# Decoder layer on one core: projections as single float32 products, expert slots filled from phase one on, cache values loaded 128 partitions wide

## The reference, cut to what matters

```python
u = x @ w_in + b_in                    # columns: lru_x 1024 | lru_y 1024 | q 1024 | k 256 | v 256 | gates 2 x 1024
rec = recurrent_branch(lru_x, lru_y)   # conv width 4, two block gates, scan over time, * gelu(lru_y)
att = window_attention(q, k, v)        # 16 heads, 4 kv heads, window 128; the samples read cache_k and cache_v
merged = sigmoid(g_l) * (rec @ w_lru_out) + sigmoid(g_a) * (att @ w_attn_out)
x1 = layer_norm(ALPHA * x + merged @ w_o)
# hierarchical MoE: best of 4 groups, two best of its 8 experts
y = layer_norm(ALPHA * x1 + sum_over_2_experts(w * (silu(x1 @ w_gate[e]) * (x1 @ w_up[e])) @ w_down[e]))
```

## Time and profile before

| | us |
|---|---|
| median of 3 runs (1116.97 to 1119.11) | 1118.64 |
| profiled execution, first to last instruction (span) | 1115.6 |
| PE busy | 936.1 |
| DVE busy | 403.5 |
| ACT busy | 267.6 |
| start of the first expert's first transpose | 593.65 |

### The profile page before, as it was taken

How to read it: one execution, slowest core, us unless ns; L and a number is a source line. 1 busy time by engine, 2 the same in 40 slices (tenths; PEclk the granted TensorE clock), 3 DMA queues, 4 the chain that set the end, 5 groups by cost and what they waited for, 6 DMA issues and landing times.

```text
span 1115.6 us, 14382 instructions
## 1 busy us (share of the span) xinstructions
PE 936.1 (84%) x5619; PEld 631.1 (57%) x5619; DVE 403.5 (36%) x874; ACT 267.6 (24%) x508; POOL 120.9 (11%) x195
## 2 busy tenths in 40 slices
PE   7999952999999999999927998888887887887844
PEld 6999952888999998978823333322222222222311
DVE  4765831776564545265561111010110011001126
ACT  3556430444344342311110111100110011011111
POOL 3000401000000000000012122011111111110003
PEclk8999985999999999999957999999999999989986
DMA  9233440211122142723494899999999999999962
GB/s 290 76 77 76 127 96 21 75 42 52 62 77 76 55 135 77 195 100 137 176 416 179 336 422 420 422 421 424 422 422 421 423 424 423 420 422 423 422 243 112
DMA packets 87896, 268.84 MB, mean 241 GB/s; under 512 B 32657, under 2 KB 59405, under 8 KB 67330
## 3 DMA queue, kind: packets, MB, share of 16 engines
q1 hardware_dynamic: 77602, 254.89, 58.8%
q0 software_dynamic: 10240, 13.21, 3.6%
HBM read 263.17 MB, written 15.16 MB: 249 GB/s over the span
## 4 chain that ended last, share of the span: by engine, by line
PE 50%; DMA 27%; DVE 10%; SPq 4%; another core or an unknown queue 3%; ACT 3%; issue 2%; POOLq 0%; POOL 0%; DVEq 0%; ACTq 0%
DMA slot<-in_w_up 26%; PE ps L764 25%; PE ps L1066 7%; PE ps L1093 5%; PE ps L981 5%; SPq L459 4%; PE ps L851 2%; PE ps L805 1%; PE ps L885 1%; DVE rawL L1450 1%; PE ps L875 1%; DVE hL L1536 1%; PE ps L1049 1%; PE ps L1001 1%
## 5 line engine op out<-in xcount | busy, mean ns | idle before, releaser
L1066 PE MATMUL ps<-slot,xt 128*64 128x512 f32 x512 | 248.3, 634 | 71.5 <-DMA slot<-in_w_up 70.5
L1067 PE MATMUL ps<-slot,xt 128*64 128x512 f32 x512 | 248.6, 635 | 0.0
L1066 PEld LDWEIGHTS ps<-slot,xt 128*64 128x64 f32 x512 | 69.3, 144 | 222.1 <-issue 152.8
L764 PE MATMUL ps<-xTh,wh 128*128 128x260 f32 x704 | 149.4, 294 | 1.5 <-DVE rawL L1450 1.5
L764 PE MATMUL ps<-xTl,wh 128*128 128x260 f32 x704 | 144.0, 287 | 0.0
L764 PE MATMUL ps<-xTh,rawL 128*128 128x260 f32 x704 | 144.0, 286 | 0.0
L1928 DVE COPY xt<-ps 128x512 f32<-128x512 f32 x32 | 22.1, 692 | 295.8 <-PE ps L1049 295.8
L1093 PE MATMUL ps<-slot,hT 128*64 128x512 f32 x512 | 116.9, 598 | 1.4 <-DVE hT L1938 1.4
L764 PEld LDWEIGHTS ps<-xTh,wh 128*128 128x128 f32 x704 | 112.4, 194 | 2.8 <-issue 1.8
L764 PEld LDWEIGHTS ps<-xTl,wh 128*128 128x128 f32 x704 | 111.5, 194 | 0.0
L764 PEld LDWEIGHTS ps<-xTh,rawL 128*128 128x128 f32 x704 | 110.9, 193 | 0.0
(11 more groups left out here) (314 smaller groups left out, 1210.2 us busy)
## 6 DMA issues: line engine op xcount, KB each, us to landing
slot<-in_w_down SPq DMA_DIRECT2D x32, 2048.0 KB, 28.7
slot<-in_w_gate SPq DMA_DIRECT2D x64, 1024.0 KB, 27.8
slot<-in_w_up SPq DMA_DIRECT2D x64, 1024.0 KB, 32.4
raw<-in_w_in SPq DMA_DIRECT2D x18, 1024.0 KB, 5.1
raw<-in_w_in SPq DMA_DIRECT2D x16, 256.0 KB, 4.5
raw<-in_w_lru_out SPq DMA_DIRECT2D x4, 1024.0 KB, 5.1
raw<-in_w_attn_out SPq DMA_DIRECT2D x16, 256.0 KB, 4.6
wo_raw<-in_w_o SPq DMA_DIRECT2D x4, 1024.0 KB, 8.6
```

What stands on the lines that cost most here:

```text
L764: last = mm(out_of[:, a, 0:HT], w[:, k, :], x[:, k, a * HT:(a + 1) * HT], start=(k == 0 and n == 0), stop=(k == KT - 1 and n == 2))
L1066: mm(out[0:CAP, :], tokens, w[:, q, :], start=start, stop=stop)
L1067: last = mm(out[CAP:P, :], tokens, w[:, 4 + q, :], start=start, stop=stop)
```

## The change

- **Products.** `passes` becomes `product`: one float32 product per block and half, 16 matmuls to a tile, straight from `raw`. `w_hi`, `w_lo`, `wo_hi`, `wo_lo` and the splits of the activations are gone, with their semaphores; ACT and DVE copy the transposed x in turns. `mix` has 16 matmuls to a token tile. The factor 0.5 that was folded into `w_o` moves into the layer norm (`2.0 * ALPHA` and a second epsilon).
- **Buffers.** `raw` has four buffers instead of three. `m1`/`mg`, `sg`, `wo`, `kwin`, `snew`, `lnG`, `lnB`, `xre` and `x1T` lie elsewhere, which leaves some expert slots free from the start or from tile 44 on.
- **Expert slots.** `chunk(0, 0, 0)` is issued behind half-chunk 8, `chunk(1, 1, 1)` and `chunk(2, 1, 1)` behind half-chunks 25 and 26, three chunks at the last merge, and expert 2's three chunks when the last token tile's sum is ready. All of `w_o` is loaded behind the last half-chunk.
- **Cache values.** `cV` is loaded 128 partitions wide; its row 0 is written afterwards, behind the conv state stores and a wait of POOL for the load. DVE's wait in `probs_t` for the stores and the loads is gone, and so is ACT's wait for the h store before the first gate tile.

```diff
-AHEAD = 3
+RAWS = 4
-for _k in range(KT):
-    _place(FIRST["ga"] + 11 + _k // 2, ("wo", _k))
...
             for hc in range(2, NT // 2):
                 half_chunk(hc)
-                if hc == 24:
-                    sp.wait_ge(s_proj, FIRST["lo"] + 12)
-                    for n in range(2):
-                        sp.dma_start(wo_raw[0][:, 2 * n:2 * n + 2, :], w_o[:, 2 * n:2 * n + 2, :]).then_inc(s_wo, 16)
+                if hc == 8:
+                    chunk(0, 0, 0)
+                if hc == FIRST["ga"] // 2 + RAWS - 1:
+                    chunk(1, 1, 1)
+                if hc == FIRST["ga"] // 2 + RAWS:
+                    chunk(2, 1, 1)
             sp.wait_ge(s_pv, NUNIT)
             sp.wait_ge(s_pa, 2 * NUNIT)
+            sp.wait_ge(s_oc_out, 16 * 9)
+            sp.wait_ge(s_oh_out, 32)
...
             x_again(1)
+            chunk(1, 0, 0)
             chunk(2, 0, 0)
             chunk(0, 1, 1)
...
                 if m == TT - 1:
-                    sp.wait_ge(s_lg, 3)
-                    chunk(0, 0, 0)
-                    chunk(1, 1, 1)
                     sp.wait_ge(s_mix, TT)
-                    chunk(1, 0, 0)
+                    chunk(0, 2, 2)
+                    chunk(1, 2, 2)
+                    chunk(2, 2, 2)
...
-            def passes(out_of, hi, lo, rhs_h, rhs_l):
+            def product(out_of, w, x):
                 last = None
                 for k in range(KT):
-                    for n, (w, x) in enumerate(((hi, rhs_h), (hi, rhs_l), (lo, rhs_h))):
-                        for a in range(2):
-                            last = mm(out_of[:, a, 0:HT], w[:, k, :], x[:, k, a * HT:(a + 1) * HT],
-                                      start=(k == 0 and n == 0), stop=(k == KT - 1 and n == 2))
+                    for a in range(2):
+                        last = mm(out_of[:, a, 0:HT], w[:, k, :], x[:, k, a * HT:(a + 1) * HT],
+                                  start=(k == 0), stop=(k == KT - 1))
...
-                pe.wait_ge(s_hi, t + 1)
-                pe.wait_ge(s_lo, t + 1)
+                if t % 2 == 0:
+                    pe.wait_ge(*raw_full(t))
...
-                    lo = woL[k // 4][:, k % 4, :]
-                    for p, (x, w) in enumerate(((mgH, woH[:, k, :]), (mgH, lo), (mgL, woH[:, k, :]))):
-                        for h in range(2):
-                            last = mm(out[0:ROWS[n], h, :], x[:, k, cols], w[:, h * 512:(h + 1) * 512],
-                                      start=(k == 0 and p == 0), stop=(k == KT - 1 and p == 2))
+                    for h in range(2):
+                        last = mm(out[0:ROWS[n], h, :], mg[:, k, cols], wo[k // 4][:, k % 4, h * 512:(h + 1) * 512],
+                                  start=(k == 0), stop=(k == KT - 1))
```

More of the change, by code:

```diff
@@ L172, in build @@
         oh = at("oh", [NS + 1, D], F32, oF + 4096)
[L173 to L176, removed]
+        raw = [at(f"raw{n}", [P, KT, 256], F32, oG + 8192 * n) for n in range(RAWS)]
         xc = [at(f"xc{n}", [P, XCW], F32, oI + 2176 * n) for n in range(2)]
@@ L292, in build @@
         s_x = [sem(f"token_tile_loaded{n}") for n in range(TT)]
-        s_raw = [sem(f"raw_loaded{n}") for n in range(3)]
+        s_raw = [sem(f"raw_loaded{n}") for n in range(RAWS)]
         s_cst = sem("constants_built")
         s_xT = sem("x_transposed")
-        s_xh, s_xl = sem("x_hi"), sem("x_lo")
+        s_xa, s_xd = sem("x_T_by_act"), sem("x_T_by_dve")
         s_vT, s_col = sem("vectors_transposed"), sem("vectors_in_columns")
@@ L328, in build @@
         s_ln = sem("ln1_loaded")
-        s_wo = sem("w_o_loaded")
+        s_wo = [sem(f"w_o_loaded{n}") for n in range(2)]
         s_mix, s_z, s_sd = sem("sum_ready"), sem("ln_stats"), sem("ln_root")
@@ L360, in raw_full @@
             hc = t // 2
-            return s_raw[hc % 3], 16 * sum(dmas(n) for n in range(hc % 3, hc + 1, 3))
+            return s_raw[hc % RAWS], 16 * sum(dmas(n) for n in range(hc % RAWS, hc + 1, RAWS))
         def emptied(t):
@@ L367, in emptied, with wcol @@
             return (s_eva if who == "act" else s_evd), n
[L369 to L374, removed]
+        def wcol(t):
+            return raw[(t // 2) % RAWS][:, :, (t % 2) * P:(t % 2 + 1) * P]
         def halves(ap):
@@ L779, in tile @@
                 kind, i = TILES[t]
-                rhs_h, rhs_l = {"lo": (recH, recL), "ao": (attH, attL)}.get(kind, (xTh, xTl))
+                rhs = {"lo": rec, "ao": att}.get(kind, xT)
                 if t == 0:
-                    pe.wait_ge(s_xl, TT)
+                    pe.wait_ge(s_xa, 3)
+                    pe.wait_ge(s_xd, 2)
                 if kind == "lo" and i == 0:
@@ L892, in cache_t @@
                     pe.wait_ge(s_ck, 16)
-                    pe.wait_ge(s_attl, 1)
+                    pe.wait_ge(s_att, 1)
                     pe.wait_ge(s_pd, 2)
@@ L1150, in _ @@
             sc = nc.scalar
-            for n in range(TT):
+            for n in range(0, TT, 2):
                 r = ROWS[n]
                 act.wait_ge(s_xT, n + 1)
[L1154 to L1162, removed]
+                sc.activation(xT[:, :, n * P:n * P + r], flat[n % 2].rearrange("p (k c) -> p k c", k=KT)[:, :, 0:r],
+                              ACT.Copy).then_inc(s_xa, 1)
             def read_tile(t):
@@ L1292, in sample_att @@
                     for p2 in range(2):
[L1293 to L1297, removed]
+                        ins = sc.activation(att[half, 4 * p2:4 * p2 + 4, SEQ:T], o[half, p2, a, :, :], ACT.Copy)
+                    ins.then_inc(s_sat, 1)
             act.wait_ge(s_lam, 1)
@@ L1327, in _ @@
                     sample_att()
-                elif what == "wo":
-                    wo_hi(*args)
             def root_of(m, before):
@@ L1334, in root_of @@
                 act.wait_ge(s_z, before + m + 1)
-                sc.activation(mv[0:r, m % 3, 2:3], mv[0:r, m % 3, 1:2], ACT.Sqrt, bias=epsT[0:r, :]).then_inc(s_sd, 1)
+                eps = epsT[0:r, 0:1] if before else epsT[0:r, 1:2]
+                sc.activation(mv[0:r, m % 3, 2:3], mv[0:r, m % 3, 1:2], ACT.Sqrt, bias=eps).then_inc(s_sd, 1)
             def x1_t(m):
@@ L1674, in read_tile @@
                     link(v.scalar_tensor_tensor(out=yb[:, :], in0=y2[:, :], scalar=1.0, in1=yb[:, :], op0=ALU.add, op1=ALU.mult))
-                    link(v.scalar_tensor_tensor(out=yb[:, :], in0=yb[:, :], scalar=0.5, in1=hL[:, i, 0:T], op0=ALU.mult, op1=ALU.mult))
-                    link(v.tensor_copy(recH[:, i, 0:T], yb[:, :]))
-                    v.tensor_tensor(recL[:, i, 0:T], yb[:, :], recH[:, i, 0:T].bitcast(F32), ALU.subtract).then_inc(s_rec, 1)
+                    v.scalar_tensor_tensor(out=rec[:, i, 0:T], in0=yb[:, :], scalar=0.5, in1=hL[:, i, 0:T],
+                                           op0=ALU.mult, op1=ALU.mult).then_inc(s_rec, 1)
                 elif kind == "lo":
@@ L1727, in _ @@
                     probs_t(*args)
-                elif what == "pv":
-                    attend(*args)
                 elif what == "sk":
```

151 lines of the change are left out of this document (48 added, 103 removed).

## The result

The changed kernel takes 1157.65 us (median of 4 runs, 1156.97 to 1161.84) against 1118.23 of the kernel before (4 runs): ratio 1.037, 95% interval 1.034 to 1.039. The prediction was 941 us, between 924 and 970. It has the wrong sign.

A forecast was written before the change was run, and what follows sets the result against it. PE was taken to bound the path up to the experts, apart from the hole, and expert weight transfer the rest. Gains 36.2 + 36 + 17 + 42.8 + 27 + 19 = 178 off 1118.64 gave 941 us, range 924 to 970.

The forecast's parts named there:

- A tile becomes 16 x 0.219 = 3.50 us: Projections on PE: 16 float32 products at 0.219 us replace 48 float32r ones, gaining 2.25 us a tile.
- a float32 product costs four float32r ones: Rival for projections and sum with w_o: 0.482 us a product, so slower, 1215 us; chance 0.03.
- The hole: PE idle from 152.74 us, before tile 20, through DVE's wait for row 0 of cV; its removal gains 36.2 us.
- The price of a load that stays slow: Cache values: a 53 us cV load would hold POOL until 157 and DVE 20 us at tile 22: 961 us.
- Phase one's walk: Stretch-by-stretch estimate of gains from start to tile 59, with the limits set by DVE and ACT taken off.
- start and tiles 0 to 19: First projections, recurrence and unit 0's scores: gain 36 us, with 10 of 46 lost to DVE; tile 20 starts near 118.5.
- tiles 20 to 28: Tiles that are round trips of ACT and DVE: nine gain 2.2 each, less 3 for the clock; gain 17 us.
- tiles 29 to 47: Projections among attention matmuls: 19 tiles gain 2.25 us each, 42.8 us, up to 6 less if units slip.
- tiles 48 to 59: Last unbroken projections of phase one: 69.47 us becomes 42, gain 27 us.
- sum, norm and routing, up to the first transpose: Sum with w_o: 4.5 token tiles on the path gain 4.2 us each, 19 us; the way after the logits stays.
- DVE and ACT keep the pace of tiles 13 to 28: Rival in phase one: only the hole is gained in those tiles, 26 us lost, 967 us; chance 0.14.
- PE sets the pace everywhere: Rival in phase one: DVE's 17 us of scans hide behind four tiles, so 927 us; chance 0.12.

## Why the prediction was wrong, point by point

**The step that failed** is "A tile becomes 16 x 0.219 = 3.50 us". The price 0.219 was right for one instruction: 7.01/32. The count was not. I took the instructions in the trace for the products in the code. The rows of before could have told: the gate step writes four products (two weight matrices, two halves), and I read "8 in 1.83" as eight of them without counting the loop. The groups of the kernel before, by form, against what the code issues (44 tiles read x, so 44 x 16 = 704 float32r products of low x by high weights; 48 scores of 256 columns; 8 gates x 2 halves = 16 products with each gate matrix):

```profile
L764 PE MATMUL ps<-xTl,wh 128*128 128x260 f32 x704 | 144.0, 287 | 0.0
...
L851 PE MATMUL ps<-kz,qT 128*128 128x256 f32 x96 | 23.2, 385 | 0.0
...
L805 PE MATMUL ps<-xc,wrg 128*128 128x272 f32 x32 | 8.7, 393 | 0.0
```

A float32r product has one row (704 for 704); a float32 one has two (96 for 48, 32 for 16). A price per instruction was multiplied with a number of products. The right working from the same rows was 4 products in 1.83 us, 0.458 for 272 columns, 0.437 for 260; a tile 16 x 0.437 = 7.0.

**The break-even was named and crossed.** The text said that the change turns slower from about 0.39 us a product on; the product costs 0.438. The rival "a float32 product costs four float32r ones", chance 0.03, is the one that came, with its price a little high: 0.438 is 3.63 times 0.1206. At the granted clock of 1.00 (2.4 GHz) 0.438 us are 4.04 clocks a column, and a float32r product takes 1.11. The Trainium skill, FP8 and Floating Point Precision, section TensorE Precision Notes, says that true FP32 makes four passes. These rows agree with it, and my sentence that the rows did not show it was wrong, since I had read half a product. The rival's 1215 us was too slow as it kept 0.482 a product and gave nothing back for stalls.

**The sum over PE.** Tiles: 60 x 1.25 = 75 us more instead of 135 less. Sum with `w_o`: 12 more (4.5 token tiles) instead of 19 less. The hole gives 36 back. 75 + 12 - 36 = 51, and the first transpose moved by 38.3: the remaining 13 or so are what PE no longer loses to others. Its idle time before the experts fell from 77.6 to 34.7 us, 42.9, of which 34.4 are the wait of the hole, so 8.5 are other stalls. The rest, some 4 us, I did not separate; the granted clock is a candidate (0.98 from 190 to 420 us in the kernel before, 1.00 in the changed one).

**The hole** (36.2): right in size (35.8 measured with the load alone). The price of a load that stays slow, 20 us, was right in its way, POOL's queue and `qz`, and no run tests its size. The 20 and the 157 belong to tiles of 3.5 us. The run with the narrow load has tiles of 7.01; POOL stood there for 55 us, until 208, and it cost 10. Nor did POOL stand at the wait that the text had in mind: that run has none.

**Phase one's walk**, tested with half the products:

| part | gain predicted | gain with half the products |
|---|---|---|
| start and tiles 0 to 19 | 36 | 31.6 (154.5 to 122.97) |
| tiles 20 to 28 | 17 | 18.4 (80.0 to 61.6) |
| tiles 29 to 47 | 42.8 | 42.0 (150.9 to 108.9) |
| tiles 48 to 59 | 27 | 27.1 (69.47 to 42.35) |
| sum, norm and routing, up to the first transpose | 19 | 19.6 (102.6 to 82.9) |
| experts | 0 | -2.4 (522.0 to 524.3) |
| whole, with 36.2 for the hole | 178 | 172.5 (spans, 1115.6 to 943.1) |

The total fits within 6 us, and so does each part within 5. What is missing lies mostly in the first part: tile 20 starts at 122.97 for a forecast of 118.5. DVE's scans ended at 110.3 for 109, and behind the gap of 4.92 us the granted clock was 0.69 (111.8 to 119.0): unit 0's scores took 2.07 us there, and the tile behind them 4.72 for 3.5. "DVE and ACT keep the pace of tiles 13 to 28" (967) and "PE sets the pace everywhere" (927) would have been wrong with these tiles.

**The early chunks and the experts**: worth 0 and 522 us; right (1157.04 for 1157.65 without the early chunks, 523.3 us for the experts).

## What to carry to other kernels

When a price per instruction is read from a trace and multiplied with a count from the code, count one known loop on both sides first: here 16 products written stood against 32 rows, and that factor of two was nearly the whole error: with half the products the kernel takes 944 us, for a forecast of 941. On these rows three float32r products (0.36 us for 260 columns) are cheaper on PE than one float32 product (0.44), so the split pays here, where PE is the bound in phase one and the other engines have room for it. The gain from a removed wait could be had alone: the wide load without the rest gives 36 us and beats both kernels.

## What the runs showed of the hardware that I had not expected

- A float32 product is two matmuls with two weight loads in the trace, each some 2 clocks a column: 0.219 us for 260 columns and 0.434 for 512, so 0.438 and 0.868 for the product; a float32r one took 0.1206 and 0.232.
- The 127-partition load of 1 MB not only landed late (53.5 to 57.1 us for the row behind it, against 8.6 to 11.8 for the load and 1.7 to 4.0 for the row in the kernels with the wide one). Where small transfers follow it directly (the kernel before, the sum alone in float32, the narrow load in the changed kernel), it stopped POOL's whole queue for 52 to 55 us after the third of them, without a semaphore, so that the profile calls this idle time "issue".
- The narrow load takes POOL 6.7 us to issue, the wide one 0.91, and the page counts 10240 packets in the software queue of the kernel before, 6432 with the wide load alone.
